# Expert gate and up weights read with four consecutive rows to a partition

## What is computed

```
x = layer_norm(ALPHA * x + mixed, ln1_g, ln1_b)          # (x - mean) / std * g + b
# each token: the best of 4 groups, the best 2 of its 4 experts, weights `combine`
h = silu(einsum('td,edf->etf', x, w_gate)) * einsum('td,edf->etf', x, w_up)
h = h * combine.T[:, :, None]
ffn = einsum('etf,efd->td', h, w_down)                   # D = 2048, D_EXPERT = 512
x = layer_norm(ALPHA * x + ffn, ln2_g, ln2_b)
```

## Time and profile before

| | us |
|---|---|
| median of three runs | 1424.29 (1422.36 to 1425.29) |
| span of the profiled execution | 1423.4 |
| PE busy | 1345.4 (95%) |
| PEld busy | 962.6 (68%) |
| DVE busy | 559.5 (39%) |
| ACT busy | 483.1 (34%) |

### The profile page before, as it was taken

One profiled execution on the slowest core, in us unless ns is written; L12 is line 12 of the kernel. 1 busy time (PEld: TensorE's weight loads), 2 busy tenths in 40 slices (PEclk: granted clock), 3 DMA queues, 4 the chain that ended last, 5 costly groups with the idle time before them and its releaser, 6 DMA issues.

```text
span 1423.4 us, 18028 instructions
## 1 busy us (share of the span) xinstructions
PE 1345.4 (95%) x7212; PEld 962.6 (68%) x7212; DVE 559.5 (39%) x695; ACT 483.1 (34%) x632; POOL 38.6 (3%) x49
## 2 busy tenths in 40 slices
PE   6999999999999999999999799799999999999994
PEld 6989989998888888888888577534343343434331
DVE  3477435456454545545445345601111010210106
ACT  3444344346546454444344233311111111211111
POOL 0000000300000000001000000000000000000002
PEclk9999999999999999999999999899999999999997
DMA  9667556544443444555565758699999999999992
GB/s 314 204 183 246 178 185 199 178 160 152 151 158 131 164 161 159 166 190 170 186 202 181 242 177 295 234 403 397 395 405 388 407 387 406 394 399 401 392 410 95
DMA packets 168778, 364.68 MB, mean 256 GB/s; under 512 B 14528, under 2 KB 20128, under 8 KB 159776
## 3 DMA queue, kind: packets, MB, share of 16 engines
q1 hardware_dynamic: 156944, 354.41, 69.9%
q10 hardware_dynamic: 11792, 9.66, 2.2%
HBM read 361.95 MB, written 2.10 MB: 256 GB/s over the span
## 4 chain that ended last, share of the span: by engine, by line
PE 92%; DVE 3%; ACT 2%; ACTq 1%; issue 1%; DMA 1%; SPq 0%; DVEq 0%
PE main L875 18%; PE main L877 18%; PE main L876 18%; PE main L416 16%; PE att L445 8%; PE att L401 5%; PE main L458 4%; PE att L1100 1%; PE att L1068 1%; ACTq L1464 1%; DMA raw<-in_w_in_dram 1%; ACT whi L1261 1%; DVE wlo L1479 1%; DVE acc L637 1%; PE att L1083 1%
## 5 line engine op out<-in xcount | busy, mean ns | idle before, releaser
L1479 DVE TENSOR_TENSOR wlo<-raw,whi 128x2048 fp32r<-128x2048 f32 (+1 forms) x141 | 324.1, 2299 | 395.4 <-ACT whi L1261 395.4
L1261 ACT ACTIVATE whi<-raw 128x2048 fp32r<-128x2048 f32 (+1 forms) x141 | 269.4, 1911 | 456.3 <-PE main L877 431.1
L416 PE MATMUL main<-mraw,xg 128*64 128x512 f32 x1024 | 225.0, 594 | 0.0
L875 PE MATMUL main<-whi,xhi 128*128 128x512 f32 (+1 forms) x544 | 203.5, 374 | 1.3 <-ACT uT L1300 1.3
L877 PE MATMUL main<-whi,xlo 128*128 128x512 f32 (+1 forms) x544 | 201.8, 371 | 0.0
L876 PE MATMUL main<-wlo,xhi 128*128 128x512 f32 (+1 forms) x544 | 201.5, 370 | 0.0
L875 PE MATMUL main<-xhi,whi 128*128 128x256 f32 (+1 forms) x560 | 160.4, 286 | 5.6 <-DVE wlo L1479 5.6
L416 PEld LDWEIGHTS main<-mraw,xg 128*64 128x64 f32 x1024 | 72.6, 137 | 134.7 <-issue 133.2
L876 PE MATMUL main<-xlo,whi 128*128 128x256 f32 (+1 forms) x560 | 159.6, 285 | 0.0
L877 PE MATMUL main<-xhi,wlo 128*128 128x256 f32 (+1 forms) x560 | 159.5, 285 | 0.0
L445 PE MATMUL att<-mraw,hT 128*64 128x512 f32 x512 | 113.0, 600 | 6.2 <-ACT hT L497 6.2
(11 more groups left out here) (299 smaller groups left out, 1309.5 us busy)
## 6 DMA issues: line engine op xcount, KB each, us to landing
raw<-in_w_in_dram SPq DMA_DIRECT2D x96, 1024.0 KB, 5.1
mraw<-in_expert_w_gate_dram SPq DMA_DIRECT2D x64, 1024.0 KB, 14.2
mraw<-in_expert_w_up_dram SPq DMA_DIRECT2D x64, 1024.0 KB, 14.5
mraw<-in_expert_w_down_dram SPq DMA_DIRECT2D x64, 1024.0 KB, 13.8
raw<-in_w_branch_dram SPq DMA_DIRECT2D x24, 1024.0 KB, 5.1
raw<-in_w_out_dram SPq DMA_DIRECT2D x16, 1024.0 KB, 5.1
xin<-in_x_dram SPq DMA_DIRECT2D x4, 512.0 KB, 5.9
xr<-in_x_dram ACTq DMA_DIRECT2D x1, 2048.0 KB, 8.0
```

The lines of the kernel that those rows point to most:

```text
L416: ins = pe.matmul(main[0][half, w, :], xg[:, k, half], unit[:, kk * DE:(kk + 1) * DE], start=(k == 0), stop=(k == KT - 1))
L875: pe.matmul(o, ah, bh, start=start, stop=False, skip_group_check=skip)
L1261: act.activation(whi[:, u % SPLIT, 0:n], raw[:, slot, 0:n], ACT.Copy).then_inc(hi_done, 1)
L1479: dve.tensor_tensor(wlo[:, u % SPLIT, 0:n], raw[:, slot, 0:n], whi[:, u % SPLIT, 0:n].bitcast(F32), ALU.subtract).then_inc(lo_done, 1)
```

## The change

A gate or up unit still has the same 512 rows, but partition p now takes the rows 4p to 4p + 3, which lie side by side in memory: one piece of 8 KB instead of four of 2 KB. The slice kk of the buffer (512 numbers) is then row 4p + kk of the unit in place of row 128 kk + p.

The stationary operand of `gate_up` has to have its rows in the same order. So `gather` takes for its k-th block not 128 neighbouring columns of `xr` but every fourth: columns q*512 + 4m + (k mod 4) for m = 0 to 127. `gate_up` itself is as it was.

LN1's gain and shift must come in that order too. The old table `gbT` stays for the router; a second one, `gbP`, is read from memory by two DMAs on SyncE's queue, ahead of the first expert unit, in pieces of four numbers (16 bytes), and ScalarE waits for it (`gbp_in`) before its loop over the pairs.

```diff
+        gbP = carve(1, "gbP", [P, 2 * KT])
...
-                return rows.rearrange("a (k p) f -> p (a k) f", p=P)
+                return rows.rearrange("a (p k) f -> p a (k f)", p=P)
...
-                dst = mraw[slot][:]
-                if r % MU < 4 * QUADS:
-                    dst = dst.rearrange("p (k f) -> p k f", f=DE)
-                else:
-                    dst = dst.unsqueeze(1)
+                dst = mraw[slot][:].unsqueeze(1)
...
             sp.wait_ge(unit_used, U1)
+            for j, name in enumerate(("ln1_g", "ln1_b")):
+                sp.dma_start(gbP[:, j * KT:(j + 1) * KT].rearrange("p (q k) -> p q k", k=4),
+                             A[name][0].rearrange("(q p k) -> p q k", p=P, k=4)).then_inc(gbp_in, 16)
...
-                            ins = pe.matmul(att[:, q, k % 4 * P:(k % 4 + 1) * P], xr[:, t, k * P:(k + 1) * P], hot[:, t, :],
+                            rows = xr[:, t, q * 512:(q + 1) * 512].rearrange("p (m k) -> p k m", k=4)[:, k % 4, :]
+                            ins = pe.matmul(att[:, q, k % 4 * P:(k % 4 + 1) * P], rows, hot[:, t, :],
...
             act.wait_ge(np_ok, 2)
+            act.wait_ge(gbp_in, 32)
...
-                                             bias=gbT[:, KT + k:KT + k + 1], scale=gbT[:, k:k + 1])
+                                             bias=gbP[:, KT + k:KT + k + 1], scale=gbP[:, k:k + 1])
```

More of the change, by code:

```diff
@@ L298, in build @@
         m_ps, m_hi, m_lo, xr_in, out_free = sems("m_ps m_hi m_lo xr_in out_free")
-        l1_in, l1_var, l1_std, l1_mul, z_ok, acc_ok, gb_in, gb_ps, gb_out = sems(
-            "l1_in l1_var l1_std l1_mul z_ok acc_ok gb_in gb_ps gb_out")
+        gbp_in, l1_in, l1_var, l1_std, l1_mul, z_ok, acc_ok, gb_in, gb_ps, gb_out = sems(
+            "gbp_in l1_in l1_var l1_std l1_mul z_ok acc_ok gb_in gb_ps gb_out")
         wr_in, br_in, gw_ok, gs_ok, gs_ps, t_ps, t_out, lt_ps, lt_out, r_ps = sems(
```

## The result

| | before | changed |
|---|---|---|
| median, us | 1423.32 (1421.75 to 1425.29, 4 runs) | 1486.99 (1484.97 to 1488.84, 4 runs) |
| span of the profiled execution, us | 1423.4 | 1487.0 |
| ratio, 95% interval | | 1.0443 (1.0424 to 1.0462) |

The change makes the kernel 4.4% slower, 63.6 us by the spans. The direction and the place were forecast; the size was not, and the time lies 5 us above the range given.

The account below looks back on a forecast made before the run. The prediction took the expert part to be bound by TensorE, with the DMA hidden by a thin margin. 1423.4 + 0 (pieces) + 0 (gbP) + 48.7 (gather's step) = 1472.1 us, given as 1473 us, range 1422 to 1482.

Parts of the forecast that it names:

- TensorE's chain, no DMA in it: Expert part: one pair's chain of waits, 61.10 us, is TensorE but for short hand-overs to ScalarE and VectorE.
- the 25 us of transfers saved beside it: Gate and up loads: 8 KB pieces save 128 x 0.20 us of DMA time, costed at zero because TensorE waits for none.
- the second table: Two gbP loads ahead of the first expert unit: 0 to 15 us to landing, hidden, so zero cost.
- the slack at the end: Last pair's down units: even at the worst they land 4 us before TensorE needs them.
- little cover: Gather: weight loads of 106 ns start 111.6 ns apart, so about 5 ns of a load's growth is hidden.
- rows of another engine at 64 and 128 bytes: VectorE operations with a step, used to price the gather's step of 16 bytes: 0.79 and 0.72 ns more a number.
- 487 x 100 ns: Gather: the step of four adds 100 ns to each of 487 full-clock weight loads, 48.7 us.
- its upper end: Gather's step: at most one further access for each column, 0.83 x 128 = 106 ns a load.
- VectorE's rows: Nearest prices for the gather's step: 0.72 to 0.79 ns extra a number, taken as an amount, 92 to 101 ns.
- A load of 206 ns: First gather: the first 25 or so loads, about 213 ns apart at the lower clock, hide the step's cost.
- a rival at 0.06: The clock falls too: each of 24 gather blocks followed by a fall of 1.42 us, 1475 to 1507 us; chance 0.06.

Follow-up runs that it names:

- the filler: Changed kernel with six more matmuls of 128 columns in each pair, results overwritten, while TensorE waits between gate_up and down: 1482.35 us.
- the filled kernels: The changed kernel and the kernel before, each with six more matmuls of 128 columns in each pair, results overwritten: 1482.35 us and 1422.92 us.

## Why the prediction was wrong

**Right: what bounds, and what is hidden.** TensorE's chain, no DMA in it; the 25 us of transfers saved beside it at zero; the second table, which landed in 5.1 us, at zero; the slack at the end, given as at least 4 us and measured as 4.8. The pieces alone show all of it at a ratio of 1.0007.

**Right: where the loss is.** At full clock the load had little cover (about 5 ns was estimated), and what the step adds goes straight onto the gather's records. That a step of 16 bytes has a price at all rested on rows of another engine at 64 and 128 bytes; it came true, but nothing in the kernel before could show it.

**Wrong: the size of the step.** The term was 487 x 100 ns = 48.7 us, with 106 ns as its upper end. The gather of a pair grew by 7.79 us, which is 121.7 ns a load. The upper end came from the thought that a step can add no more than one access at the load's own pace, 0.83 ns a column. The price of opening a new stretch is not bounded by that: 1.82 ns, as at steps two, three and four. VectorE's rows, at 0.72 to 0.79 ns extra on 1.0, are 1.7 to 1.8 ns in all for a number, close to the same figure. I carried over the difference; the total, 128 x 1.8, would have given 230 ns. That is hindsight: no run shows that the two engines pay for the same thing, and the rows compared there differ in more than the step (L713 sums groups of 16, L1627 takes the maximum over 256).

This term is the step that failed. With the load as measured and without the falls in the down products the time is 1482.35 us, as with the filler, already at the upper end of the range; with the falls and the load as forecast it would have been about 1478, inside it.

**Wrong: the first gather.** A load of 206 ns was held to be covered by the 213 ns of the lower clock. The load takes 233 ns, at that clock as at the other, and is not covered: the double block took 6.51 us and takes 7.73. The three blocks of the first pair are 15.59 against 10.47 us, 5.1 more, not 39 x 0.1 = 3.9.

**Wrong: the clock.** I had it as a rival at 0.06 and put its cause in the half-empty gather. It happened, but the falls that cost are at the hand-over between gate_up and down, the same place as the one before, and with that place filled the profiled execution has none there and the median is 4.6 us lower. Why they are more frequent in the changed kernel is open. In the expert part the profiled executions with a step of four or eight show three to seven of them (the step alone three, the changed kernel six, the step of eight seven), those with whole gathers and steps of one to three none or one, and the filled kernels one and none. Each is one execution, and no run varied the length of a pair by itself.

The sum by the measured terms:

| | forecast, us | measured, us |
|---|---|---|
| gather, pairs 2 to 8: 7 x 64 loads | 44.8 | 7 x 7.79 = 54.5 |
| gather, pair 1 | 3.9 | 5.1 |
| falls of the clock in the down products | 0 | 118.3 - 113.0 = 5.3 |
| start of the first gather | 0 | 909.71 - 910.91 = -1.2 |
| pieces, table, wait | 0 | 0 |
| sum | 48.7 | 63.7 (spans: 63.6) |

## What to carry to other kernels

Before a layout is chosen for the DMA's sake, look at what reads it: a float32 stationary operand with a step of two costs almost nothing, with a step of four it doubles the distance between loads, and beside matmuls of 128 moving columns a load has next to no cover. For 128 columns the time of a load can be worked out in advance: for neighbours at most 112 ns (106 by the estimate of 0.83 ns a column), and otherwise 1.82 ns for each 16 bytes opened, where that is more. And a saving in transfers that nobody waits for is worth what the bound engine later gives up: here nothing, and 15 us as soon as TensorE's part was 28 us shorter.

## What the runs showed of the hardware that was not expected

- A strided load is not slower by a share but has a floor of its own: 64, 96 and 128 stretches of 16 bytes take 117.7, 174.5 and 232.6 ns, and the 232.6 ns stand beside matmuls of 128 and of 256 columns.
- The strided load does not follow TensorE's clock: at a granted clock of 0.50 its starts are 233 ns apart as at full clock, while those of neighbours go from 112 to 213 ns, the matmuls' own pace.
- With six short matmuls of no use in a hand-over of 3 us the profiled execution had one fall of the clock in place of six, and the median was 4.6 us lower.
- The DMA engines move pieces of 8 KB at one unit in 2.48 us, of 4 KB in 2.56 and of 2 KB in 2.71, with a share of about 1.0 for both ends.
